# Hybrid decoder trunk on one core: two weight tiles of the projection loaded ahead of the decays' store, and the first chunk's inverse placed two places later

## The reference

```
h = rms_norm(x, norm1);  proj = h @ w_in
sb = stick_breaking_attention(sb_q, sb_k, sb_v)               # 4 heads x 64
dn = gated_delta_rule(l2(q), l2(k), v, g, beta)               # 4 heads x 128, behind a causal conv of 4 taps and silu
hg = hgrn2_recurrence(silu(hg_q), hg_k, hg_i, log_f)          # 4 heads, 64 x 64 state
x = x + concat(norm(sb), norm(dn)*silu(z), norm(hg)*sigmoid(g)) @ w_out
x = x + (silu(h2 @ w_gate) * (h2 @ w_up)) @ w_down;  return rms_norm(x, final_norm)
```

## Time and profile before

| | us |
|---|---|
| median of 3 runs (lowest to highest) | 1453.78 (1453.25 to 1461.49) |
| the profiled execution, its own time | 1453.09 |
| its span | 1451.2 |
| PE busy / weight loads / DVE / ACT / POOL | 1397.7 / 1171.3 / 738.3 / 542.0 / 617.0 |
| granted clock of TensorE, mean | 0.995 |

### The profile page before, as it was taken

The page is one execution under the profiler, slowest core; times in us unless marked ns, Lnnn a source line. Parts: engine busy times, 40 slices in busy tenths (PEclk is TensorE's granted clock), DMA queues, the critical chain, the costliest instruction groups (busy, mean ns, idle before and its releaser), DMA issues.

```text
span 1451.2 us, 24659 instructions
## 1 busy us (share of the span) xinstructions
PE 1397.7 (96%) x9457; PEld 1171.3 (81%) x9457; DVE 738.3 (51%) x1288; ACT 542.0 (37%) x1293; POOL 617.0 (43%) x552
## 2 busy tenths in 40 slices
PE   5969999999999999998999999999999999999997
PEld 4757897988888888887887788888888888888886
DVE  5014535556354688876147843533535335354436
ACT  6123545445342545543133423223232232332435
POOL 3123324133243566661301946346354463543650
PEclk9989999999999999999999999999999999999999
DMA  5031313323225322524210022121221211302103
GB/s 176 9 108 39 108 49 94 120 70 115 61 81 149 108 89 75 158 79 149 59 29 1 29 58 63 54 58 34 55 81 36 59 51 37 88 30 58 59 29 131
DMA packets 122003, 106.52 MB, mean 73 GB/s; under 512 B 6352, under 2 KB 107296, under 8 KB 121888
## 3 DMA queue, kind: packets, MB, share of 16 engines
q1 hardware_dynamic: 121744, 104.43, 23.5%
q10 hardware_dynamic: 144, 0.52, 0.1%
HBM read 83.95 MB, written 20.99 MB: 72 GB/s over the span
## 4 chain that ended last, share of the span: by engine, by line
PE 89%; DVE 4%; POOL 2%; issue 2%; DMA 1%; ACT 1%; SPq 0%; DVEq 0%; POOLq 0%; ACTq 0%
PE banks L2290 9%; PE banks L2292 9%; PE banks L2291 9%; PE banks L326 6%; PE banks L328 5%; PE banks L327 5%; PE banks L2307 5%; PE banks L2308 5%; PE banks L2309 5%; PE banks L658 2%; PE banks L2076 2%; PE banks L2078 2%; PE banks L2077 2%; PE banks L659 2%; PE banks L660 2%
## 5 line engine op out<-in xcount | busy, mean ns | idle before, releaser
L2414 POOL TENSOR_TENSOR w_l<-area,w_h 128x512 fp32r<-128x512 f32 x102 | 143.4, 1412 | 195.8 <-ACT w_h L2327 195.8
L2414 POOL TENSOR_TENSOR w_l<-w_raw,w_h 128x512 fp32r<-128x512 f32 x86 | 118.2, 1378 | 165.3 <-ACT w_h L2327 165.3
L2558 DVE TENSOR_TENSOR area<-area,banks 128x512 f32<-128x512 f32 x176 | 121.0, 687 | 120.7 <-PE banks L2309 118.3
L326 PE MATMUL banks<-act_h,w_h 128*128 128x512 f32 x352 | 142.3, 404 | 13.3 <-POOL w_l L314 13.3
L328 PE MATMUL banks<-act_h,w_l 128*128 128x512 f32 x352 | 138.1, 392 | 0.0
L327 PE MATMUL banks<-act_l,w_h 128*128 128x512 f32 x352 | 138.0, 392 | 0.0
L314 POOL TENSOR_TENSOR w_l<-w_raw,w_h 128x1024 fp32r<-128x1024 f32 x24 | 59.3, 2475 | 156.3 <-ACT w_h L307 139.1
L2307 PE MATMUL banks<-w_h,ff_h 128*128 128x512 f32 x320 | 124.6, 389 | 0.0
L2290 PE MATMUL banks<-act_h,w_h 128*128 128x512 f32 x320 | 124.6, 389 | 0.0
L2309 PE MATMUL banks<-w_h,ff_l 128*128 128x512 f32 x320 | 124.6, 389 | 0.0
L2292 PE MATMUL banks<-act_h,w_l 128*128 128x512 f32 x320 | 124.6, 389 | 0.0
(11 more groups left out here) (303 smaller groups left out, 3306.7 us busy)
## 6 DMA issues: line engine op xcount, KB each, us to landing
w_raw<-in_w_in SPq DMA_DIRECT2D x22, 512.0 KB, 4.0
area<-in_x SPq DMA_DIRECT2D x8, 1024.0 KB, 8.1
projected_tm<-area SPq DMA_DIRECT2D x32, 256.0 KB, 2.3
w_raw<-in_w_gate SPq DMA_DIRECT2D x12, 512.0 KB, 4.5
area<-in_w_down SPq DMA_DIRECT2D x12, 512.0 KB, 3.9
w_raw<-in_w_up SPq DMA_DIRECT2D x12, 512.0 KB, 4.7
projected_cm<-area SPq DMA_DIRECT2D x20, 256.0 KB, 2.2
area<-projected_tm SPq DMA_DIRECT2D x8, 640.0 KB, 5.6
```

What stands on the lines that cost most here:

```text
L326: e.matmul(dst, w_h[:, b, k], act_h[:, k, cols], start=(k == 0), stop=False)
L2414: e.tensor_tensor(slot(w_l, u), raw_use(u), slot(w_h, u).bitcast(F32), ALU.subtract).then_inc(sems["fl"], 1)
L2558: e.tensor_tensor(dst, dst, bank(4 + (16 * p + c) % 4), ALU.add).then_inc(sems["x_added"], 1)
```

## The change

The loads of tiles 4 and 5 are issued from `first_sync`, before the decays' store and the gain rows. The load of tile 6 stands behind that of the first row weights. On PE the eight pieces from `m_turn(0)` to `update(0, 5)`, with the `pack`s and `turn`s between them, stand two places later; the last, `update(0, 6)`, one place later. On ACT `inverse(0, 2)`, and on DVE `pack(0, 3)` and `update(0, 3)`, move from the end of unit 1 to the start of what is done at the end of unit 2.

```diff
@@ first_sync
             for w in range(2, W_P1):
                 load_tile(e, w, w % 2, first_tile(w))
+            for w in range(W_P1, W_P1 + 2):
+                lead_tile(e, w)
@@ lead_sync
-            for w in range(W_P1, W_P1 + 3):
-                lead_tile(e, w)
             load_rows_of(e, 0)
+            lead_tile(e, W_P1 + 2)
@@ mixer_pe, beside(unit, point)
-                if unit == 1 and point == 1:
+                if unit == 1 and point == 3:
                     e.wait_ge(sems["o_evac"], nend - 1)
                     m_turn(0)
-                if unit == 1 and point == 2:
+                if unit == 1 and point == 4:
                     e.wait_ge(sems["wt_ready"], NH)
                     pack(0, 1)
                     turn(0, 0)
...
-                if unit == 2 and point == 4:
+                if unit == 2 and point == 6:
                     pack(0, 6)
                     turn(0, 5)
-                if unit == 2 and point == 6:
+                if unit == 2 and point == 7:
                     update(0, 6)
@@ mixer_act, beside(unit), unit 1
                     inverse(0, 1)
+                if unit == 2:
                     inverse(0, 2)
-                if unit == 2:
                     inverse(0, 3)
```

More of the change, by code:

```diff
@@ L1449, in beside @@
                     turn(0, 0)
-                if unit == 1 and point == 3:
+                if unit == 1 and point == 5:
                     update(0, 1)
-                if unit == 1 and point == 4:
+                if unit == 1 and point == 6:
                     turn(0, 1)
                     pack(0, 2)
-                if unit == 1 and point == 5:
+                if unit == 1 and point == 7:
                     update(0, 2)
-                if unit == 1 and point == 6:
+                if unit == 2 and point == 0:
                     pack(0, 3)
                     turn(0, 2)
-                if unit == 1 and point == 7:
+                if unit == 2 and point == 1:
                     update(0, 3)
-                if unit == 2 and point == 0:
+                if unit == 2 and point == 2:
                     turn(0, 3)
                     pack(0, 4)
-                if unit == 2 and point == 1:
+                if unit == 2 and point == 3:
                     update(0, 4)
-                if unit == 2 and point == 2:
+                if unit == 2 and point == 4:
                     turn(0, 4)
                     pack(0, 5)
-                if unit == 2 and point == 3:
+                if unit == 2 and point == 5:
                     update(0, 5)
-                if unit == 2 and point == 4:
+                if unit == 2 and point == 6:
                     pack(0, 6)
                     turn(0, 5)
-                if unit == 2 and point == 6:
+                if unit == 2 and point == 7:
                     update(0, 6)
```

## The result

| | before | after |
|---|---|---|
| median, us | 1455.57 (4 runs, 1453.25 to 1461.49) | 1436.92 (4 runs, 1436.83 to 1437.29) |
| profiled execution, its own time / span, us | 1453.09 / 1451.2 | 1437.29 / 1435.4 |

The ratio is 0.9866, with a 95% interval of 0.9835 to 0.9898: faster, by 1.3%. The forecast was 1437.5 us within 1434.8 to 1441.5. It was made against the first three runs of the kernel before; a fourth came out at 1457.36 and moved that median. The two medians lie 18.65 us apart, which is more than the change explains: executions of the kernel before scatter upwards, as the experiments show. So the gain is best compared in the traces: 16.27 us forecast, 15.80 (1.1%) between the two profiled executions.

A forecast was written before the change was run, and what follows sets the result against it. PE was taken to bound the kernel, busy 1397.7 of 1451.2 us, its longest single wait 13.3 us for tile 4. Gains 14.85 + 1.42 = 16.27 us give 1436.8 profiled, median 1437.5; range 1434.8 to 1441.5.

The forecast's parts named there:

- Loads earlier, the stall gone: Start of the projection stage: PE's first product with tile 4 starts at 70.68 instead of 83.95, gaining 13.27 us.
- The slow first steps: First nine steps with tile 4: 2.17 us instead of 3.75 at the lower clock, gaining 1.58 us.
- No new wait behind the moved loads: Early projection stage: SP's wait for tile 3's split costs nothing, and tiles 5 and 6 cause PE no wait.
- The inverse: Unit 1, last row run: twelve more products ahead of `m_turn` remove its 1.05 us wait, leave 0.2 at `pack`; gain 1.42 us.
- The last `update` fits: `update(0, 6)`, one place later: asked for at 469.6, DVE's copy done at 469.01, ACT's at 469.23; fits by 0.4 us.
- All is kept to the end: First step to end: L1234 comes near 481.0 - 16.3 = 464.7, and the shift there is the shift at the end.
- The slower rival: Projection stage: without a pause the granted clock drops to 1.2 GHz over 88 to 200; 1484.5 us, chance 0.02.

The follow-up runs named there:

- e1: The kernel before with only the loads of tiles 4, 5 and 6 moved, the inverse left where it was; 1439.18 us, ratio 0.9885.
- e4: The changed kernel with the load of tile 6 ahead of the row weights, not behind them; 1438.13 us.
- e2: The changed kernel with the load moves taken back, so that only the inverse is moved; 1452.92 us, ratio 0.9981.
- e8: The changed kernel with POOL's `causal(0)` moved behind `values(0)`, away from DVE's first `update`; 1438.27 us.
- e7: The changed kernel with every inverse piece behind `m_turn(0)` one place later still, `update(0, 6)` in unit 3; 1436.67 us.
- e3: The changed kernel with tiles 4 and 5 issued right behind the decays' store, still ahead of the gain loads; 1440.47 us.
- e6: The changed kernel with the inverse pieces only one place later than in the kernel before, not two; 1437.26 us.
- e9: The kernel before, unchanged, run again with a trace; profiled execution 1455.18 us, median of ten runs 1455.06 us.
- e5: The changed kernel itself, unchanged, run once more as its second set; 1437.55 us, ratio 0.9865.
- e11: The kernel before, unchanged, one more execution with a trace; profiled execution 1457.98 us.
- e10: The kernel before, unchanged, one more execution with a trace; profiled execution 1453.78 us.

## Why the prediction was right, and where it was off

1. *Loads earlier, the stall gone*: as forecast, 13.27 us. Measured 83.95 - 70.92 + 0.42 = 13.45, since the first product follows the scores at 0.10 us and not, as I took it, at 0.28.
2. *The slow first steps*: forecast 1.58, measured 3.75 - 2.15 = 1.60. Together 14.85 forecast, 15.09 found, 15.08 in e1.
3. *No new wait behind the moved loads*: right for the wait of SP, for tile 5 and for tile 6, whose split starts 0.2 us from where it was put, and whose place in the queue does not matter (e4).
4. *The inverse*: forecast 1.42, measured 1.20, and 1.37 in e2 and e4. The step was right, with a residual of 0.31 at `pack` where 0.2 was forecast. What I had taken as fixed, the end of L1774's chain, moved by 0.16: in the changed kernel's trace DVE's first `apart` piece (L1659 at 429.10) took 1.82 beside POOL, and its second 0.43; before it was 0.69 and 1.40. In both traces DVE's and POOL's pieces start in the same hundredth of a us; which of them takes the longer varies from trace to trace, and so does the end, by 0.2 us. e8 shows that the `update`'s length came of POOL's work beside it, as the Trainium skill has it ("SBUF — State Buffer", "Who interferes with whom"; the trace agrees, 0.29 against 0.74). The missing 0.22 is thus 0.16 at `pack` and 0.08 at the last `update`, less rounding. With the wait at `pack` gone the move gives 31.56 - 29.98 = 1.58 (e7), about the upper bound of the forecast (1.6).
5. *The last `update` fits*: it does, but the cover of 0.4 us that was forecast was not there. Asked for at 469.6 in the clock of before, it was asked for at 469.8; DVE's copy, put at 469.01, ended at 454.75 + 0.41 + 14.67 = 469.83. DVE had been held ahead of it by L1659 (0.91 us) and L288 (1.15), which took 0.68 and 0.43 before: POOL now worked beside them. So this step came out right by luck, at a price of 0.08 us.
6. *All is kept to the end*: right, -15.87 at the first step and -15.8 at the end.
7. *The slower rival*, the clock falling in the projection stage for want of a pause. It did not come: from 21 to 782 us the granted clock of the changed kernel is 1.00 throughout.

The forecast of 1437.5 lies 0.6 above the first median and 0.05 below the second set's. The gain of the loads was 0.24 more than forecast and that of the inverse 0.22 less, and 0.42 was lost at the start of the kernel, which was not in the sum at all. The mechanism is the one forecast; that the time comes so near is in part luck, since these errors partly cancel, and so is which executions had falls.

## What to carry to other kernels

When PE waits for a weight tile, follow the wait through the splitting engines to the DMA, and from the DMA's landing to its issue: here the tile was free to load 26 us earlier, and a run of small broadcast loads ahead of it in one queue cost more than five times what the semaphore ahead of them did. Work that is woven into a busy engine's stream is placed by the end of what it waits for; each group moved ahead of the waiting instruction gives its own length and no more, up to the wait. Compare variants by distances between the same instructions in the traces, for in medians differences of a us drown in the falls of the clock.

## What the runs showed that was not expected

The granted clock falls to 0.50 for 3 to 7 us also where PE had waited no more than 2.1 us at a time, and not in every execution. The first step of the changed kernel and of e7 has the same instructions; in e7 its length was 28.05 us, in the changed kernel 26.54. It begins with the L1235 at 465.14 in the one (464.16 in e7) and ends with the next step's. The stretches of the changed kernel, then of e7:

```profile
469.00:471.00 2.00, 1.80 (x28) 1.64 (x30) 1.49 (x6) 0.02 (x1) 0.98 (x2) 1.00 0.83 188
471.00:473.00 2.00, 2.00 (x40) 1.85 (x40) 0.29 (x1) 1.27 (x3) 1.23 (x4) 1.00 0.95 363
```

```profile
468.00:470.00 2.00, 1.77 (x21) 1.71 (x22) 1.51 (x6) 0.00 (x0) 0.96 (x2) 0.65 0.76 195
470.00:472.00 2.00, 2.00 (x25) 1.78 (x26) 0.00 (x0) 0.60 (x1) 1.25 (x4) 0.50 0.96 364
```

PE had waited 0.82 us at L1224 in both, at 469.20 in the changed kernel and at 468.23 in e7, but the clock fell in e7 alone. Such a fall in the first step stands in the traces of e2, e3, e6, e7 and e8, one in the last full step (25.6 us instead of 24.2) in e1, e4 and e9, and others later, near 664 to 674 us and near 784 (16 to 20 us later in the kernel before and e2). What one costs depends on what PE has to wait for next. In the steps it is 1.4 to 1.5 us, and in e8 at 674 1.4. Near 664 (e1, e4, e5, e9, e11) only 0.3 to 0.5 us of the loss are left 8 us later. The one near 784 stands in every trace but those of e8, e10 and the kernel before, and it costs nothing. The changed kernel's own trace has it, with the columns of the stretches above:

```profile
782.00:784.00 2.00, 2.00 (x5) 1.59 (x6) 2.00 (x1) 2.00 (x2) 2.00 (x1) 0.56 0.00 0
```

PE loses some 1.6 us in it and gets them back at its next waits for POOL's splits. PE's waits there, before and then after:

```profile
797.75 0.50 PE L2235 MATMUL banks<-act_h,w_h 128*128 128x512 f32 x1 [2.09 <-POOL w_l L2414]
804.34 0.50 PE L2235 MATMUL banks<-act_h,w_h 128*128 128x512 f32 x1 [0.81 <-POOL w_l L2414]
...
828.18 0.50 PE L2290 MATMUL banks<-turns,w_h 128*128 128x512 f32 x1 [1.78 <-POOL w_l L2414]
```

```profile
781.98 0.61 PE L2236 MATMUL banks<-act_h,w_h 128*128 128x512 f32 x1 [2.09 <-POOL w_l L2415]
...
812.41 0.50 PE L2291 MATMUL banks<-turns,w_h 128*128 128x512 f32 x1 [1.31 <-POOL w_l L2415]
```

The shift is 15.77 us at 797.75 and 15.77 at 828.18, so this fall takes nothing from the comparison of the two traces. Together the falls are as large as the differences between these variants. Which execution gets one, no run here tells: the same waits stand ahead of it where the clock fell and where it did not (0.82 us in e7 and the changed kernel, 1.2 in e11 and e10, 2.1 near 784 after and before).
